# High parts made in the middle of a pair of chunks, and modulation columns one step later, in a three-pass fp32r transformer kernel

## The chip, the cores and the metric

One core of one Trainium2 chip runs the kernel. The metric is device time in microseconds (us); the number before is the median of three runs. Lower is better.

## The reference, cut to what matters

A sequence of 512 rows with 1024 features passes through two hybrid layers, then a pooling layer and a dilated attention layer, each with a gated feed-forward part. All of it is dense fp32 products with small attention parts between them:

```python
mod = c_act @ w_ada + b_ada                 # 6 x 1024 columns: shift, scale, gate, twice
h = modulate(rms_norm(x, norm1_g), shift1, scale1)
(rq, rk, rv, rg, gq, gk, gv, glr, gg, fq, fk, fv, ff) = split(h @ w_in)
ret = silu(rg) * head_group_norm(retention(...))
gla_o = silu(gg) * rms_norm(gla(...))
fox_o = forgetting_attention(rms_norm(fq), rms_norm(fk), fv, ff + b_fox_f)
x = x + gate1 * (sum(gates * y_br) @ w_o)
x = x + gate2 * ((silu(conv(u)) * g) @ w_down)
...
o, lse = dilated_window_attention(q, k, v, window, dilation)    # last layer, 16 heads
```

## The kernel before, in words

**Weights.** They are streamed as numbered chunks of at most 128x1024 fp32 (512 KB). Chunk n uses slot n % 6 of `raw`, `hi` and `lo` (`raw` and `lo` are the same memory). SyncE issues the DMA of chunk n once TensorE (or, for chunks of `w_ada`, VectorE) is done with the earlier chunk in that slot (L2610). ScalarE writes the high part to `hi` (`ScalarSteps.split`, L1211, instruction L1220) after waiting for the DMA to land. GpSimd subtracts to get the low part (L2596). TensorE forms every product in three passes, high x high, high x low, low x high (L427 to L429).

**How far ahead.** Each time the ScalarE program takes a chunk n (`ScalarSteps.chunk`, L1222), it first splits everything up to n + AHEAD, with AHEAD = 4. The split waits in ScalarE's own instruction order: while its DMA is on the way, nothing behind it on ScalarE runs.

**Pairs.** Where rows are wanted instead of columns (values and the gated part's keys), two chunks na and nb = na + 1 are used together (`project_rows`, L479 for TensorE, L1249 for ScalarE). Both slots come free only at the end of the pair. A pair has eight steps of 12 matmuls; the ScalarE part evicts the first bank (`take(0)`) after step four and the second after step eight. A pair can't start in slot 5, so now and then a chunk number is left out. There are 15 pairs, seven in each of the two hybrid layers and one in the last attention layer: two for retention's values, two for the fox values (chunks 45 and 48 in layer 0, 271 and 273 in layer 1), three for the gated part (chunks 50, 52, 54 and 276, 278, 280; `gla_inputs`, L800) and chunk 495 in `attn_inputs` (L1042, ScalarE L1674).

**Order of work.** Every engine runs the same `schedule` (L321) over its own steps. `weave(main, fill)` makes one step of an attention part and then one of a projection. The fox attention has 19 steps n, after four of `fox_norm`; `gla_inputs` is its fill, so the middles of its three pairs fall at n = 0, n = 8 and n = 16, their starts before n = 0, at n = 4 and at n = 12. In a step n TensorE does `score(n)` (L753), `turn(n - 2)` (a transpose of the normalised scores, L764) and, at n = 6, 10, 14 and 18, `value` (L774, instruction L779), which needs ScalarE's copies `foxT` (L1447) up to `turned(n - 3)`. ScalarE does `exp(n)` (L1436), `turned(n - 2)` (L1442), then the fill's step. VectorE does `top(n)` (L2126), then `scale(n - 1)` (L2135, instruction L2140), for which TensorE's `turn` waits. The end of `ret_attention` runs over the first pair of fox values: after the sums (L505) ScalarE takes a root (`rstd`, L1257, instruction L1260), VectorE a reciprocal (L2060), and TensorE spreads it (`head_rows`, L509, instruction L517).

**Modulation.** For columns 4 to 11 of layer 0 and all twelve of layer 1 the product with `w_ada` runs on VectorE beside other work (`VectorSteps.ada`, L1949): four chunks of two multiply-adds (L1965), eight steps in all. After the last come a transpose (L1978) and a sum (L1980) into `AS`. TensorE then folds `AS` into a bank with four small fp32 products (`ada_fold`, L612, instruction L618), and VectorE adds the bias (`ada_add`, L1933, instruction L1938). Both come at the start of the step that begins the next column, and VectorE's first multiply of the next column (L1962) waits for the fold. Banks are taken in a fixed rotation of two, three or four (`take_bank`, L415); the fold takes one turn of it.

Of the kernel before, what the change touches and what calls it, by code (L numbers as in the profile page):

```python
# [21 lines left out]
AHEAD = 4  # L22
# [101 lines left out]
class Mark:  # L124


    def __init__(self, sem, step=1):
        self.sem, self.step, self.n, self.table, self.sure = sem, step, 0, {}, False
# [187 lines left out]
def qk_jobs():  # L316

    return [job for p in range(8) for job in (("aq", p, 128 * p), ("ak", p, 1024 + 128 * p))]


def schedule(P):  # L321
# [15 lines left out]
    for l in range(DEPTH):  # L337
# [4 lines left out]
        ada = (y for q in range(4, 12) for y in P.ada(0, q)) if l == 0 else iter(())  # L342
        P.order = ["b0", "b1"]
        weave(P.ret_attention(l), beside(P.fox_inputs(l), ada, 16))
        P.order = BIG3
        fill = P.gla_inputs(l)
# [3 lines left out]
        fill = chain(P.gated(l, 0), P.mixing(l, 0, (0, 2)))  # L350
        weave(P.gla_attention(l), fill)
        drain(beside(P.gated(l, 1), ada, 8))
        P.order = BIG4
        drain(beside(chain(P.mixing(l, 0, (1,)), *[P.mixing(l, dp, (0, 2, 1)) for dp in (1, 2, 3)]), ada, 26))
        P.mods(l, 1)
        drain(P.out_proj("w_o", l, P.x_norm(2 * l + 1)))
# [40 lines left out]
class TensorSteps(Steps):  # L397


    def __init__(self, e, K):  # L400
        super().__init__(e, K)
        self.free = {b: None for b in K.bank}
        self.order, self.turn = BIG3, 0

    def chunk(self, parts, width, split=True, pair=False, tag=None):
        n = self.next_chunk(pair)
        self.K.chunks[n] = dict(parts=parts, width=width, split=split, tag=tag)
        return n
# [70 lines left out]
    def project_rows(self, ap, c0, keys, freed, rows=None):  # L479

        t, m = self.t, self.m
        na = self.weight(ap, 0, 8, c0, 128, pair=True)
        nb = self.weight(ap, 0, 8, c0 + 128, 128)
        assert nb == na + 1 and na % NSLOT != NSLOT - 1
        hi, lo = self.K.slot_pair(na)
        for u in range(2):
            b = self.take_bank(keys[u])
            for i in range(2):
                r = 2 * u + i
                pick = slice(r * 128, r * 128 + 128) if rows is None else rows(r)  # L490
                terms = [(t["HH"][:, k, pick], t["HL"][:, k, pick], hi[:, :, k, :], lo[:, :, k, :], self.h_ready(k))
                         for k in range(8)]
                done = [] if i == 0 else [keys[u]] + ([("chunk", na), ("chunk", nb)] if u else [])
                yield from self.dot(self.bank[b][:, i * 256:i * 256 + 256], terms, done,
                                    (m.lo.at(na), m.lo.at(nb), self.free[b]))
            self.free[b] = freed(u)
# [108 lines left out]
    def ada(self, l, q_):  # L605
        for g in range(4):
            self.ada_chunk(l, q_, g)
            yield None
            yield None
        self.ada_fold(l, q_)  # L610

    def ada_fold(self, l, q_):  # L612

# [589 lines left out]
class ScalarSteps(Steps):  # L1203
# [43 lines left out]
            take(i)  # L1247

    def project_rows(self, take):  # L1249
        self.chunk(pair=True)  # L1250
        self.chunk()
        for u in range(2):
            for _ in range(4):
                yield None
            take(u)

    def rstd(self, st, n, width, ready, out, key):  # L1257

        self.q.wait_ge(ready)
        self.e.activation(out, st[:, 0:n], ACT.Sqrt, bias=self.t["eps"][:, 0:1], scale=1.0 / width).then_inc(*key)  # L1260
# [413 lines left out]
    def attn_inputs(self):  # L1674
        e, q, m, t = self.e, self.q, self.m, self.t
        jobs = qk_jobs()
        turned = []

        def rope(i):
            name, p, _ = jobs[i]  # L1680
            self.rope((name, p), 32, 64 ** -0.5 if name == "aq" else 1.0, t["aT"][:, i % 2, :],
                      m.vtake.at(*jobs[i - 2][0:2]) if i >= 2 else None, m.vtake.at("cosine", name, p))

        def keep_rows(u):
            key = ("av", 0, u)
            q.wait_ge(m.dense.at(*key))
            e.activation(t["av"][:, 2 * u:2 * u + 2, 0:256],
                         self.bank[self.K.where.get(key, "b0")][:, :].rearrange("p (t c) -> p t c", t=2),
                         ACT.Copy).then_inc(*m.atake.up(key))

        def keep_tile(p):
            out = self.bank[self.K.where.get(("avt", p), "b0")]
            q.wait_ge(m.dense.at("avt", p), m.attn.at("avr", p - 1) if p > 2 else None)
            if p < 3:
                a = e.activation(t["aV"][:, :], out[:, :], ACT.Copy)
            else:
                a = e.activation(t["aV"][:, :].rearrange("p (r l) -> p r l", r=4),
                                 out[:, :].rearrange("p (l r) -> p r l", r=4), ACT.Copy)
            a.then_inc(*m.atake.up(("avt", p)))

        def turn_values():
            for p in turned:
                q.wait_ge(m.attn.at("avr", p))
                e.activation(t["av"][:, :, p * 128:p * 128 + 128],
                             self.bank[self.K.where.get(("avr", p), "b0")][:, :].rearrange("p (t c) -> p t c", t=4),
                             ACT.Copy).then_inc(*m.atake.up(("av", p, 0)))
            turned.clear()

        def begin(i):
            if i < 2:  # L1710
                rope(i)
            else:
                keep_tile(2)
                turned.append(2)

        yield from self.projects(range(3), 6, begin)
        for what, p, *rounds in ATTN_ORDER:
            if what == "vv":
                self.chunk(pair=True)
                self.chunk()  # L1720
                for i in range(8):
                    if i == 5:
                        turn_values()
                    if i % 4 == 3:
                        keep_rows(i // 4)
                    yield 1 if i >= 8 - rounds[1] else 0
                continue
            self.chunk()
            if p > 1:
                turn_values()  # L1730
            yield rounds[0]
            if what == "v":
                keep_tile(p)
                turned.append(p)
            else:
                rope(2 * p + "qk".index(what))
            yield rounds[1]
        turn_values()
# [82 lines left out]
class VectorSteps(Steps):  # L1821


    def __init__(self, e, K):
        super().__init__(e, K)
        self.late = None

    def out_of(self, key):
        return self.bank[self.K.where.get(key, "b0")]
# [119 lines left out]
    def ada(self, l, q_):  # L1949
        e, q, m, t = self.e, self.q, self.m, self.t  # L1950
        AA, CA = t["AA"], t["CA"]
        for g in range(4):
            n = self.next_chunk()
            raw = self.K.raw[:, n % NSLOT, :]
            if n in self.K.chunks:
                q.wait_ge(*self.K.loaded(n))
            for k in range(2):
                kk = 2 * g + k
                done = [("ada", l, q_, kk)] + ([("chunk", n)] if k and g < 3 else [])
                if kk == 0:  # L1960
                    q.wait_ge(m.anorm.at("ca"), m.stat.at("col", *((l, q_ - 1) if q_ else (l - 1, 11))))
                    a = e.tensor_scalar(AA[:, :], raw[:, 0:512], CA[:, 0:1], None, ALU.mult)  # L1962
                else:
                    q.wait_ge(m.vnorm.at("ada", l, q_, kk - 1))
                    a = e.scalar_tensor_tensor(out=AA[:, :], in0=raw[:, k * 512:k * 512 + 512], scalar=CA[:, kk:kk + 1],  # L1965
                                               in1=AA[:, :], op0=ALU.mult, op1=ALU.add)
                a.then_inc(*m.vnorm.up(*done))
            if g == 3:
                self.ada_sums(l, q_, n, raw[:, 0:512])
            yield None  # L1970
            yield None
        self.ada_add(l, q_)

    def ada_sums(self, l, q_, n, room):

        e, q, m, t = self.e, self.q, self.m, self.t
        q.wait_ge(m.vnorm.at("ada", l, q_, 7))
        e.transpose(room, t["AA"][:, :]).then_inc(*m.vnorm.up(("ada", l, q_, "t")))  # L1978
        q.wait_ge(m.vnorm.at("ada", l, q_, "t"))
        e.tensor_reduce(t["AS"][:, :], room.rearrange("p (b i) -> p b i", i=32), AXX, ALU.add).then_inc(  # L1980
            *m.vnorm.up(("ada", l, q_, "s"), ("chunk", n)))

# [863 lines left out]
```

## Time and profile before

| what | value |
|---|---|
| median of 3 runs | 2996.48 us (2991.75 to 2998.78) |
| the profiled execution, own time | 2995.28 us |
| its span in the trace | 2993.5 us |
| TensorE matmul busy | 2936.0 us, 98% of the span |
| VectorE / ScalarE / GpSimd busy | 1071.3 / 1090.1 / 1176.5 us |
| granted TensorE clock | 0.994 of full speed |
| HBM read | 310.61 MB, 104 GB/s over the span |

Times of rows are in microseconds from the span's start, unless marked ns. "PE" is TensorE, "PEld" its weight load, "DVE" VectorE, "ACT" ScalarE, "POOL" GpSimd, "SP" SyncE. L1220 is line 1220 of the kernel. A matmul's end is modelled, so consecutive matmuls overlap in the records.

### The profile page before, as it was taken

How to read it: one execution, taken by the hardware profiler on the slowest of the kernel's cores; microseconds unless marked ns; L12 is line 12 of the kernel's file. 1: busy time of each engine (PE TensorE's matmuls, PEld its weight loads, DVE VectorE, ACT ScalarE, POOL GpSimd, SP SyncE). 2: the span in 40 equal slices, each digit the busy share in tenths (PEclk: the TensorE clock that was granted, in tenths of full speed). 3: DMA queues.
4: the chain of work that ended last, by engine and by line, in shares of the span. 5: the costliest groups of instructions: out<-in, count | busy, mean ns of one | idle time of the engine just before them, and what ended most of it. 6: DMA issues, size and time to landing. Idle time of an engine off the chain costs nothing.

```text
span 2993.5 us, 36662 instructions
## 1 busy us (share of the span) xinstructions
PE 2936.0 (98%) x15563; PEld 2449.8 (82%) x15563; DVE 1071.3 (36%) x1862; ACT 1090.1 (36%) x1657; POOL 1176.5 (39%) x502
## 2 busy tenths in 40 slices
PE   7999999999999999999999999999999999999999
PEld 4877878898888888788898888988888877888887
DVE  2544365256664633232142220342110266521102
ACT  3424433343332433442244332333222266432221
POOL 1432235334445433234434444434444333344442
PEclk9999999999999999999999999999999999999999
DMA  6332244335555422233333333333333322233332
GB/s 214 99 99 64 75 152 154 92 115 188 193 186 177 113 76 59 61 85 95 98 90 101 98 91 97 96 92 98 93 97 97 88 82 67 72 98 94 96 97 73
DMA packets 523799, 315.09 MB, mean 105 GB/s; under 512 B 15954, under 2 KB 496884, under 8 KB 523380
## 3 DMA queue, kind: packets, MB, share of 16 engines
q1 hardware_dynamic: 523636, 312.75, 35.5%
q8 instruction: 123, 2.02, 0.3%
q14 instruction: 40, 0.33, 0.0%
HBM read 310.61 MB, written 2.10 MB: 104 GB/s over the span
## 4 chain that ended last, share of the span: by engine, by line
PE 93%; DVE 3%; DMA 2%; ACT 1%; issue 0%; SPq 0%; DVEq 0%; ACTq 0%
PE b L427 21%; PE b L429 21%; PE b L428 21%; PE o L427 5%; PE o L428 5%; PE o L429 5%; DMA raw<-in_w_in_dram 2%; PE b L468 1%; PE b L469 1%; PE b L470 1%; PE b L586 1%; PE o L779 1%; PE s L662 1%; PE b L957 1%; PE b L958 0%; PE b L959 0%
## 5 line engine op out<-in xcount | busy, mean ns | idle before, releaser
L2596 POOL TENSOR_TENSOR lo<-raw,hi 128x1024 fp32r<-128x1024 f32 (+1 forms) x492 | 1174.4, 2395 | 1778.7 <-ACT hi L1220 1778.0
L427 PE MATMUL b<-HH,hi 128*128 128x512 f32 x1792 | 713.8, 398 | 3.3 <-DVE rq L2008 3.0
L429 PE MATMUL b<-HH,lo 128*128 128x512 f32 x1792 | 699.0, 390 | 0.0
L428 PE MATMUL b<-HL,hi 128*128 128x512 f32 x1792 | 698.6, 390 | 0.0
L1220 ACT ACTIVATE hi<-raw 128x1024 fp32r<-128x1024 f32 (+1 forms) x492 | 508.9, 1039 | 462.1 <-DMA raw<-in_w_down_dram 105.8
L427 PEld LDWEIGHTS b<-HH,hi 128*128 128x128 f32 x1792 | 336.8, 188 | 83.1 <-issue 12.1
L428 PEld LDWEIGHTS b<-HL,hi 128*128 128x128 f32 x1792 | 337.0, 188 | 71.1 <-issue 2.2
L429 PEld LDWEIGHTS b<-HH,lo 128*128 128x128 f32 x1792 | 336.6, 188 | 71.2
L427 PE MATMUL b<-FH,hi 128*128 128x512 f32 (+1 forms) x594 | 218.0, 367 | 0.0
L428 PE MATMUL b<-FL,hi 128*128 128x512 f32 (+1 forms) x594 | 217.1, 365 | 0.0
L429 PE MATMUL b<-FH,lo 128*128 128x512 f32 (+1 forms) x594 | 217.1, 365 | 0.0
L427 PE MATMUL o<-HH,hi 128*128 128x512 f32 x480 | 187.1, 390 | 0.0
L428 PE MATMUL o<-HL,hi 128*128 128x512 f32 x480 | 186.8, 389 | 0.0
L429 PE MATMUL o<-HH,lo 128*128 128x512 f32 x480 | 186.8, 389 | 0.0
L2301 DVE TENSOR_TENSOR CB<-CB,b 128x512 f32<-128x512 f32 x71 | 48.9, 688 | 352.6 <-PE b L429 339.3
L1609 ACT ACTIVATE FH<-CB 128x512 fp32r<-128x512 f32 x88 | 55.6, 632 | 251.3 <-DVE CB L2301 251.3
L427 PE MATMUL b<-hi,HH 128*128 128x256 f32 x480 | 140.9, 294 | 0.0
L1965 DVE SCALAR_TENSOR_TENSOR AA<-raw,CA,AA 128x512 f32<-128x512 f32 x140 | 135.2, 965 | 4.3
L428 PE MATMUL b<-lo,HH 128*128 128x256 f32 x480 | 136.7, 285 | 0.0
L429 PE MATMUL b<-hi,HL 128*128 128x256 f32 x480 | 136.5, 284 | 0.0
L427 PEld LDWEIGHTS b<-FH,hi 128*128 128x128 f32 x594 | 112.0, 189 | 18.1
L429 PEld LDWEIGHTS b<-FH,lo 128*128 128x128 f32 x594 | 112.0, 189 | 18.1
(464 smaller groups left out, 4494.2 us busy)
## 6 DMA issues: line engine op xcount, KB each, us to landing
raw<-in_w_ada_dram SPq DMA_DIRECT2D x96, 512.0 KB, 5.0
raw<-in_w_up_dram SPq DMA_DIRECT2D x88, 512.0 KB, 4.0
raw<-in_w_in_dram SPq DMA_DIRECT2D x80, 512.0 KB, 4.2
raw<-in_w_mg_dram SPq DMA_DIRECT2D x48, 512.0 KB, 3.8
raw<-in_ffn_w_gate_dram SPq DMA_DIRECT2D x44, 512.0 KB, 3.8
raw<-in_ffn_w_up_dram SPq DMA_DIRECT2D x44, 512.0 KB, 3.8
raw<-in_w_down_dram SPq DMA_DIRECT2D x32, 512.0 KB, 4.0
raw<-in_ffn_w_down_dram SPq DMA_DIRECT2D x32, 512.0 KB, 3.9
```

The costliest lines, as they stand in the source:

```text
L427: e.matmul(out, wh, xh, start=start and k == 0, stop=False)
L428: e.matmul(out, wh, xl, start=False, stop=False)
L429: mm = e.matmul(out, wl, xh, start=False, stop=stop and k == last)
L468: e.matmul(out[:, c], hi[:, k, :], t["HH"][:, k, c], start=(k == 0), stop=False)
L469: e.matmul(out[:, c], hi[:, k, :], t["HL"][:, k, c], start=False, stop=False)
L470: mm = e.matmul(out[:, c], lo[:, k, :], t["HH"][:, k, c], start=False, stop=(k == 7))
L586: mm = e.matmul(out[0:1, :], t["CA"][:, kk:kk + 1], raw[:, k * 512:k * 512 + 512], start=(kk == 0), stop=(kk == 7))
L1220: e.activation(t["hi"][:, c % NSLOT, 0:w], K.raw[:, c % NSLOT, 0:w], ACT.Copy).then_inc(*m.hi.up(c))
L1609: e.activation(t["FH"][:, f, :], CB[:, b, :], ACT.Copy).then_inc(*m.atake.up(("fh", i, f)))
L1965: a = e.scalar_tensor_tensor(out=AA[:, :], in0=raw[:, k * 512:k * 512 + 512], scalar=CA[:, kk:kk + 1], in1=AA[:, :], op0=ALU.mult, op1=ALU ...
L2301: e.tensor_tensor(CB[:, b, :], CB[:, b, :], self.out_of(key)[:, :], ALU.mult).then_inc(*m.vtake.up(key))
L2596: e.tensor_tensor(t["lo"][:, s, 0:w], K.raw[:, s, 0:w], t["hi"][:, s, 0:w].bitcast(F32), ALU.subtract).then_inc(*m.lo.up(n))
```

## The change

On ScalarE, `project_rows` and the pair of `attn_inputs` no longer split up to nb + 4 when the pair starts. They split up to nb + 2 at the start, and the rest after the first bank's eviction, in the middle. In `attn_inputs` this is after `turn_values()` at i == 5. The fold and the addition of a modulation column are made one step later, after the first `yield` of the next column; the last column of a layer is folded at its end as before. VectorE's first multiply of a column no longer waits for TensorE's fold of the column before; the sum into `AS` does instead.

```diff
@@ TensorSteps @@
-            yield None
-            yield None
-        self.ada_fold(l, q_)
+            yield None
+            if g == 0:
+                self.ada_last()
+            yield None
+        self.unfolded = (l, q_)
+        if q_ == 11:
+            self.ada_last()
+
+    def ada_last(self):
+
+        if self.unfolded is not None:
+            self.ada_fold(*self.unfolded)
+            self.unfolded = None
@@ ScalarSteps.project_rows @@
-        self.chunk(pair=True)
-        self.chunk()
+        self.next_chunk(pair=True)
+        n = self.next_chunk()
+        self.split(n + AHEAD - 2)
         for u in range(2):
             for _ in range(4):
                 yield None
             take(u)
+            if u == 0:
+                self.split(n + AHEAD)
@@ ScalarSteps.attn_inputs @@
-                self.chunk(pair=True)
-                self.chunk()
+                self.next_chunk(pair=True)
+                n = self.next_chunk()
+                self.split(n + AHEAD - 2)
                 for i in range(8):
                     if i == 5:
                         turn_values()
+                        self.split(n + AHEAD)
@@ VectorSteps.ada: the same ada_last with ada_add, and @@
-                    q.wait_ge(m.anorm.at("ca"), m.stat.at("col", *((l, q_ - 1) if q_ else (l - 1, 11))))
+                    q.wait_ge(m.anorm.at("ca"), m.stat.at("col", 0, 3) if (l, q_) == (0, 4) else
+                              m.vnorm.at("ada", *((l, q_ - 1) if q_ else (l - 1, 11)), "s"))
@@ VectorSteps.ada_sums @@
-        q.wait_ge(m.vnorm.at("ada", l, q_, "t"))
+        q.wait_ge(m.vnorm.at("ada", l, q_, "t"), m.stat.at("col", *((l, q_ - 1) if q_ else (l - 1, 11))))
```

## Rows read from the trace of the kernel before

**Rows 1.** The page: busy time by engine, and the chain that ended last by engine.

```profile
PE 2936.0 (98%) x15563; PEld 2449.8 (82%) x15563; DVE 1071.3 (36%) x1862; ACT 1090.1 (36%) x1657; POOL 1176.5 (39%) x502
...
PE 93%; DVE 3%; DMA 2%; ACT 1%; issue 0%; SPq 0%; DVEq 0%; ACTq 0%
```

**Rows 2.** TensorE's waits: who waited for whom, us in total, times, longest.

```profile
PE o L779 <- ACT foxT L1447: 10.4, 4, 2.7
...
PE t L517 <- DVE retR L2060: 3.4, 2, 2.3
...
PE b L618 <- DVE AS L1980: 2.3, 2, 1.2
PE o L749 <- ACT foxC L1434: 2.1, 2, 1.5
```

**Rows 3.** The chain in time, 254 to 263 us: start, length, what.

```profile
254.00 0.12 PE b L429
...
254.92 5.34 DMA raw<-in_w_in_dram
...
260.28 1.06 ACT hi L1220
...
262.36 0.70 PE o L779
```

**Rows 4.** Timeline around 209 us, ScalarE, then TensorE; idle before in brackets.

```profile
209.53 1.06 ACT L1220 ACTIVATE hi<-raw 128x1024 fp32r<-128x1024 f32 x1 [3.40 <-DMA raw<-in_w_in_dram]
210.49 0.35 ACT L1260 ACTIVATE retR<-t,eps 128x128 f32<-128x128 f32 x1
...
211.88 0.38 PE L517 MATMUL t<-retR,CON 32*128 32x128 f32 x2 [2.26 <-DVE retR L2060]
```

**Rows 5.** Timeline of ScalarE in layer 1, before the second foxC copy.

```profile
1170.61 1.06 ACT L1220 ACTIVATE hi<-raw 128x1024 fp32r<-128x1024 f32 x1 [0.42 <-DMA raw<-in_w_in_dram]
```

**Rows 6.** Timeline of VectorE, then TensorE, at a late fold.

```profile
414.74 0.69 DVE L1980 TENSOR_REDUCE AS<-raw 128x16 f32<-128x512 f32 x1
...
415.48 0.25 PE L618 MATMUL b<-AS,CON 128*32 128x4 f32 x8 [1.23 <-DVE AS L1980]
```

**Rows 7.** Timeline of VectorE, then GpSimd, 258.5 to 265 us.

```profile
262.06 2.50 DVE L2140 TENSOR_SCALAR foxP<-foxP,foxD 128x256 f32<-128x256 f32 x1
...
259.75 4.66 POOL L2596 TENSOR_TENSOR lo<-raw,hi 128x1024 fp32r<-128x1024 f32 x2 [14.82 <-ACT hi L1220]
```

**Rows 8.** Timeline where the splits go, steps n = 0 to 4, 8 to 10, 16 to 18.

```profile
248.28 0.58 ACT L1475 ACTIVATE gk<-b 128x512 f32<-128x512 f32 x1
...
253.86 0.42 DVE L2140 TENSOR_SCALAR foxP<-foxP,foxD 128x384 f32<-128x384 f32 x1
...
254.60 0.29 PE L769 MATMUL t<-CON,foxP 128*128 128x128 f32 x1
...
272.88 0.59 ACT L1484 ACTIVATE gv<-b 128x512 f32<-128x512 f32 x1
...
274.59 0.29 DVE L2140 TENSOR_SCALAR foxP<-foxP,foxD 128x128 f32<-128x128 f32 x1
...
276.25 0.27 PE L769 MATMUL t<-CON,foxP 128*128 128x128 f32 x1
...
298.76 0.59 ACT L1484 ACTIVATE gv<-b 128x512 f32<-128x512 f32 x1
...
301.48 0.59 PE L779 MATMUL o<-foxT,fv 128*128 128x512 f32 x1
```

**Rows 9.** Timeline of the last layer's pair: ScalarE, GpSimd, TensorE.

```profile
2415.34 2.01 ACT L1220 ACTIVATE hi<-raw 128x1024 fp32r<-128x1024 f32 x2
...
2418.48 1.28 ACT L1750 ACT_TABLE_LOAD   x1
...
2416.48 4.88 POOL L2596 TENSOR_TENSOR lo<-raw,hi 128x1024 fp32r<-128x1024 f32 x2 [4.80 <-ACT hi L1220]
...
2422.03 0.33 PE L1117 MATMUL t<-CON,aP 128*128 128x128 f32 x1 [0.22 <-DVE aP L2446]
```

More of the change, by code:

```diff
@@ L608, in ada @@
             yield None
+            if g == 0:
+                self.ada_last()
             yield None
-        self.ada_fold(l, q_)
+        self.unfolded = (l, q_)
[4 more added lines that the diff above has]
+            self.ada_fold(*self.unfolded)
+            self.unfolded = None
     def ada_fold(self, l, q_):
@@ L1826, in __init__ @@
         self.late = None
+        self.unfolded = None
     def out_of(self, key):
@@ L1970, in ada, with ada_last @@
             yield None
+            if g == 0:
+                self.ada_last()
             yield None
-        self.ada_add(l, q_)
+        self.unfolded = (l, q_)
+        if q_ == 11:
+            self.ada_last()
+    def ada_last(self):
+        if self.unfolded is not None:
+            self.ada_add(*self.unfolded)
+            self.unfolded = None
     def ada_sums(self, l, q_, n, room):
```

## The prediction, made before any run of the change

> **What bounds the kernel now.** The first page parts to read are busy time and the chain that ended last. TensorE is busy for 2936.0 of 2993.5 us and holds 93% of the chain [rows 1]. So nothing but time in which TensorE stands still can be won, 57.5 us in all, much of it at the start. The next view is TensorE's waits. Four kinds concern this change: `value` of the fox attention waits for ScalarE's `foxT` (10.4 us in 4 places), the retention spread for a reciprocal (3.4 in 2), the fold for `AS` (2.3 in 2), the second bias product for `foxC` (2.1 in 2) [rows 2].
>
> The chain in time tells what stands behind the first. At 254.9 a weight DMA is issued, at the start of a gated pair; it lands at 260.26, and only then does ScalarE make a high part, and behind it the copy for which TensorE starts late, at 262.36 [rows 3]. ScalarE was not short of time: it stood in order behind a chunk that TensorE needs four chunks later. The same happens at the start of the third pair, and twice in layer 1. At 209.5 it is the root of the retention sums that stands behind such a split: idle for 3.40 us until the DMA landed, a high part, a root of 0.35, a reciprocal, and TensorE 2.26 us late [rows 4]. In layer 1 the first `foxC` copy stands behind the third of three splits, ended at 1171.67 [rows 5]. At 415.48 the fold waited 1.23 us for the sum that VectorE began at 414.74 [rows 6].
>
> **What the change takes away.** The high parts that are moved are needed at the earliest after the pair, so at the pair's start nobody misses them, and in its middle their DMAs have landed. The removed waits:
> - `foxT`: all 10.4 us [rows 2]. The starts of pairs two and three then hold no split.
> - The retention spread: all 3.4 us [rows 2]. Between the sums and the spread TensorE has at least 24 matmuls of the pair, 24 x 0.12 = 2.9 us [rows 3]; root, reciprocal and the way to TensorE take 211.88 - 210.49 = 1.4 [rows 4].
> - The fold: all 2.3 us [rows 2]. It comes a whole step of the projection later, at least 12 matmuls of 0.12 us or more, against waits of at most 1.2.
> - `foxC`: of 2.1 us the longest is 1.5, the other 0.6 [rows 2]. The 0.6 is the copy itself between two uses of one bank and stays. Pair 276 follows a left-out number and must still split one chunk at its start, but it no longer waits for the third: 0.8 goes.
> - A stalled matmul also loses its overlap: the steps in a running chain are 0.12 us [rows 3], a small product is 0.27 long [rows 8], so 0.15 at each of 8 stalls, 1.2.
>
> Together 10.4 + 3.4 + 2.3 + 0.8 + 1.2 = 18.1 us.
>
> **What it adds.** No instruction is new; the same high parts, low parts, folds and DMAs run. SyncE's queue keeps its order and its waits, since a slot is freed by TensorE or VectorE and not by a split. GpSimd's queue keeps its order too. But two high parts, 2.01 us together, and two low parts, 4.88 [rows 9], now fall into the middle. Behind the high parts stand `exp`, `turned` and, through them, VectorE's `scale`; beside the low parts a VectorE operation may be blocked. The row for that: `scale` is 0.42 us long at 253.86 [rows 8] and 2.50 at 262.06, just as long as GpSimd's second low part, of two that ran from 259.75 to 264.41 [rows 7]. I take it that a `scale` that begins inside a low part ends after it.
> - First gated pair (n = 0). The splits follow the copy at 248.28 and end near 250.9, the low parts run from 250.0 to 254.7. The `scale` of 253.86 would end at 254.7 + 0.4 = 255.2, and TensorE wants it at 254.60 [rows 8]: 0.6 us.
> - Second (n = 8). The splits follow the copy at 272.88, the first low part begins near 274.5 and ends near 276.9. The `scale` of 274.59 would end at 277.2, TensorE wants it at 276.25 [rows 8]: 1.0 us. If it slips in ahead of the low part this is 0.1 (`turned` is then late instead). I take 1.0, as row 7 began its operation in the same instant as GpSimd and lost.
> - Third (n = 16). The last `scale` is past. The splits follow the copy at 298.76 and end at 301.3; the last `turned`, 0.6 long, ends at 301.85 and TensorE wants it at 301.48 [rows 8]: 0.35 us.
> - Both layers: 2 x 1.95 = 3.9 us.
> - The last layer's pair. Here the splits at 2415.34 waited for no DMA; nothing is won. They now stand ahead of the table load of 1.28 at 2418.48 [rows 9], at 2418.4 to 2420.4. The first `exp` ends 1.9 us later, at 2422.5. The low parts run from 2419.5 to 2424.4, and VectorE's two scalings (0.5) end at 2425.0, where TensorE wanted them at 2422.03 [rows 9]: 3.0 us. Without the block it would be 1.2. I take 3.0: the scalings would begin well inside.
> - The other eight pairs have no attention in their second half, and no cost if the low parts are in time. The nearest is pair 45: half a pair is 48 x 0.12 = 5.8 us, copy, high part and low part about 4.2. With those 1.6 us of cover gone TensorE would wait for `lo`.
> - The folds. TensorE's work is the same, 0.25 us each [rows 6], 20 of them. They now come at the end of a tile, so VectorE adds the column before it evicts that tile, some 0.5 us later. With three or four banks in turn this is hidden behind the next tile's 24 matmuls. In the stage with two banks the next tile waits for just that eviction: 0.2 us, once. Bounds: nothing, and 20 x 0.25 = 5 us.
>
> **The sum.** -18.1 + 3.9 + 3.0 + 0.2 = -11.0 us. The profiled execution took 2995.28, so 2984.3 for its like; it stands 1.2 under the median of 2996.48, so the forecast for the median is 2985.5 us. The unknown is the cost of the collisions: from below 0, if all of it is hidden (-18.1), from above a whole blocked operation in each of seven pairs.
>
> **A page against the change.** What rows 7 show is one operation. The Trainium skill, SBUF — State Buffer, section "Who interferes with whom", makes a rule of it: VectorE operations in a two-port mode, or with two SBUF inputs, and GpSimd exclude each other for a whole instruction, whoever issues first. By that rule every pair whose middle meets attention pays; that rival is worked out below from rows, and the trace agrees with the rule at 262.06.
>
> **Rivals.**
> 1. All hidden. The moved parts find gaps, as ScalarE idles for over half of its time [rows 1]. -18.1: 2978.4. Against it: `scale` and `turned` have under 1 us of slack at n = 8 and n = 16. Chance 0.13.
> 2. No change. The stall only moves: each of the six gated pairs costs one blocked operation, 2.5 us [rows 7], and the last layer 3.0. 15.0 + 3.0 - 18.1 = -0.1: 2996.4. For it: the moved work is exactly what stood in the way before. Against it: in the third pair no `scale` is left to be blocked. Chance 0.12.
> 3. Slower. Place: the middles of the six gated pairs and of the last layer's. Mechanism: a `scale` starts behind a low part, loses a whole 2.5 us, and the late high part costs its 0.96 besides (half of 2.01 [rows 9]): 7 x 3.5 = 24.5, less 18.1: +6.4, 3002.9. It decides from 18.1 / 7 = 2.6 us a pair on. Against it: where I can place the operations, it is 0.4 to 1.0 in the gated pairs. Chance 0.05.
> 4. The change does only half of what it says: behind ScalarE's wait stands another, such as the transpose or `scale`, that ends nearly as late. Half of 10.4 + 3.4 stays: +6.9 on the forecast, 2992.4. Against it: at 259.5 the transposes before `value` had long run. Chance 0.08.
>
> My forecast has 0.62.
>
> **How the numbers follow.** The likeliest case gives 2985.5, by itself from 2981 to 2990 (collisions between 3 and 11 us; three runs of before lie 7 us apart). The range takes in all hidden below, 2978, and most of the half case above, 2993; no change and slower are left out, 0.17 together. A measurement of this kernel can tell about 0.2%, 6 us: faster means below 2990.5. That is the forecast (0.62), all hidden (0.13) and a part of the half case (0.05): 0.80. Same: the rest of the half case and no change, 0.15. Slower: 0.05.
>
> **What would show each step.** In TensorE's waits the row L779 <- `foxT` should fall from 10.4 to about 1, L618 <- `AS` and L517 <- `retR` should go, L749 <- `foxC` should stand near 1.3. New or longer rows: L769 <- `foxP` some 3 us, L1117 <- `aP` about 3 us more. ScalarE's high parts in the pairs should show no idle time for a DMA in the middle. In the trace of GpSimd and VectorE a `foxP` scaling of about 2.5 us should stand near n = 2 and n = 8. I am wrong if TensorE waits for `lo` after a pair, if the L779 wait stays, or if the last layer's first transpose is late by much more than 3 us.

## The result, and the profile after

The changed kernel takes 2977.02 us (median of 6 runs, 2976.43 to 2977.35), the kernel before in the same comparison 2995.96 (6 runs, 2991.75 to 2998.78): ratio 0.9939, 95% interval [0.9929, 0.9948]. It is faster, by 18.9 us. The forecast was 2985.5, 11 us faster, with a range down to 2978.0: the sign was right, the size was not, and the result lies 1 us outside the range. The runs of after also lie within 1 us of each other, those of before within 7.

First the page of after: the span, the busy times and the chain by engine.

```profile
span 2975.5 us, 36681 instructions
PE 2930.4 (98%) x15563; PEld 2445.2 (82%) x15563; DVE 1065.4 (36%) x1862; ACT 1087.8 (37%) x1657; POOL 1173.9 (39%) x502
PE 95%; DVE 3%; ACT 1%; DMA 1%; issue 0%; SPq 0%; DVEq 0%; ACTq 0%
```

The span fell by 2993.5 - 2975.5 = 18.0 us. Against [rows 1] this splits in two. TensorE stands still for 2975.5 - 2930.4 = 45.1 us instead of 57.5: 12.4 less. And it is busy for 5.6 us less, though it does the same matmuls. The forecast had only the first kind.

TensorE's waits of after (waiting line, releaser, us in total, times, longest), the lines that answer to [rows 2] and two that are new or longer:

```profile
PE t L1128 <- DVE aP L2473: 5.0, 6, 2.4
...
PE t L780 <- DVE foxP L2167: 1.6, 4, 0.6
...
PE o L760 <- ACT foxC L1448: 1.4, 2, 0.7
...
PE o L790 <- ACT foxT L1461: 0.2, 1, 0.2
```

The waits for `retR` and `AS` are gone, `foxT` is 0.2 instead of 10.4, `foxC` 1.4 instead of 2.1. The scales `foxP` cost 1.6 and the last layer's `aP` 5.0, where it was 2.9 before. So the queue did what was forecast. (L1128, L780, L760 and L790 are L1117, L769, L749 and L779 of before.)

Most of the other 5.6 us is in a view that the forecast had not read stretch by stretch: the granted clock. Four stretches of the kernel **before** (window, its length, TensorE busy, weight load, VectorE, ScalarE, GpSimd, then granted clock, DMA share, GB/s):

```profile
212.00:216.00 4.00, 4.00 (x44) 3.77 (x45) 2.29 (x4) 0.00 (x0) 1.01 (x1) 0.57 0.00 0
262.40:266.80 4.40, 4.40 (x14) 3.15 (x15) 2.36 (x2) 1.27 (x4) 2.01 (x1) 0.62 0.00 0
1217.80:1222.40 4.60, 4.58 (x15) 3.49 (x16) 0.68 (x2) 1.32 (x4) 2.28 (x1) 0.65 0.00 0
2502.00:2506.00 4.00, 4.00 (x14) 3.17 (x14) 1.86 (x3) 3.33 (x9) 0.54 (x1) 0.58 0.10 31
```

and the like of the kernel **after**, behind the retention spread, around the third pair's `value` in layer 1, and late in the last layer:

```profile
209.00:213.00 4.00, 4.00 (x72) 3.68 (x62) 2.38 (x4) 0.00 (x0) 0.00 (x0) 1.00 0.00 0
...
1215.00:1219.00 4.00, 4.00 (x20) 3.28 (x19) 0.00 (x0) 0.46 (x1) 0.00 (x0) 1.00 0.76 197
...
2485.00:2489.00 4.00, 4.00 (x13) 2.98 (x11) 1.74 (x3) 2.53 (x7) 1.37 (x1) 0.57 0.00 0
```

A mean of 0.57 over 4.00 us means that TensorE ran most of it at 1.2 GHz, half of its 2.4, and lost 4.00 x (1 - 0.57) = 1.7 us. The other three rows of before give 4.40 x 0.38 = 1.7, 4.60 x 0.35 = 1.6 and 4.00 x 0.42 = 1.7. The first three of the four stretches of before stand directly behind waits that the change removes: the spread released at 211.88, and `value` at 262.36 and in the third pair of layer 1. They are gone; the fourth, which has no long wait ahead of it, is still there. The chain of before shows it step by step:

```profile
214.17 0.21 PE b L428
214.38 0.21 PE b L429
...
215.85 0.12 PE b L427
215.97 0.12 PE b L428
```

The same kind of matmul takes 0.21 us a step until 215.85 and 0.12 from there on.

**The whole account.** Set each matmul of before beside the same one of after. The difference of their starts is the lead of after. It grows and shrinks like this (us):

| place | lead, change of it | forecast |
|---|---|---|
| stalls for `foxT`, four | 2.87 + 2.70 + 2.84 + 3.01 = +11.4 | +11.0 (10.4 and 4 overlaps) |
| stalls for `retR`, two | 2.33 + 1.24 = +3.6 | +3.7 |
| folds, two | 1.3 + 1.1 = +2.4 | +2.6 |
| `foxC` in layer 1 | +0.8 | +0.8 |
| stretches at 1.2 GHz that are gone, three | 1.5 + 1.6 + 1.6 = +4.7 | none |
| middles of the six gated pairs | -0.34 - 0.82 - 0.41 in each layer = -3.1 | -3.9 |
| the last layer's pair | -2.2 | -3.0 |
| `foxC`'s product at 259.65 in layer 0, behind VectorE's `EfL` (ends at 259.60) | -0.2 | none |
| an eviction one bank late | nothing seen | -0.2 |
| the rest, from the start-up and the end | +0.6 | none |
| sum | +18.0 | +11.0 |

This is one execution of each kernel. The mean granted clock is on record for each execution: 0.996 or 0.997 in all six of after, 0.992 to 0.996 with a median of 0.994 in the 39 of before beside the experiments. A difference of 0.002 is 6 us of 2990, known to some 3 us, as the clock is given to three places. So the gain by the clock is no accident of the two traces, though its 4.7 us are measured in these two alone.

### The profile page after: what moved, and what is told of

The parts are those of the page before. It is cut to its first block, busy times and chain, and to the rows that moved or that the text cites. A ratio compares the mean times of both kernels' runs of the same rounds, so it can differ in the third digit from the quotient of the medians.

```text
span 2975.5 us, 36681 instructions
## 1 busy us (share of the span) xinstructions
PE 2930.4 (98%) x15563; PEld 2445.2 (82%) x15563; DVE 1065.4 (36%) x1862; ACT 1087.8 (37%) x1657; POOL 1173.9 (39%) x502
## 4 chain that ended last, share of the span: by engine, by line
PE 95%; DVE 3%; ACT 1%; DMA 1%; issue 0%; SPq 0%; DVEq 0%; ACTq 0%
PE b L428 22%; PE b L430 21%; PE b L429 21%; PE o L428 5%; PE o L430 5%; PE o L429 5%; PE b L469 1%; PE b L470 1%; PE b L471 1%; PE b L587 1%; PE o L790 1%; PE s L673 1%; PE s L770 1%; PE b L968 1%; PE b L970 0%; PE b L969 0%
## 5 line engine op out<-in xcount | busy, mean ns | idle before, releaser
L1983 DVE SCALAR_TENSOR_TENSOR AA<-raw,CA,AA 128x512 f32<-128x512 f32 x140 | 128.7, 919 | 3.8
L429 PEld LDWEIGHTS b<-FL,hi 128*128 128x128 f32 x594 | 112.0, 189 | 18.1
L430 PEld LDWEIGHTS b<-FH,lo 128*128 128x128 f32 x594 | 112.0, 188 | 18.1
```

The costliest lines, as they stand in the source:

```text
L429: e.matmul(out, wh, xl, start=False, stop=False)
L430: mm = e.matmul(out, wl, xh, start=False, stop=stop and k == last)
```

## Experiments

Each kernel is timed against the kernel before on the same chip. The runs came in three groups: e1 to e4 (before: 2994.12 us, 13 runs), e5 to e8 (2995.29, 17 runs), e9 and e10 (2995.12, 9 runs). A stretch "at 1.2 GHz" is read from rows like those above; the long one at the start-up and the one at the end, which all kernels have, are not counted.

### e1: the last layer's pair put back

```diff
-                self.next_chunk(pair=True)
-                n = self.next_chunk()
-                self.split(n + AHEAD - 2)
+                self.chunk(pair=True)
+                self.chunk()
...
                         turn_values()
-                        self.split(n + AHEAD)
```

> The changed kernel with the last layer's pair put back: its two high parts are made at the pair's start again. Theory A (the last layer's part of the change only costs): TensorE's wait L1128 <- aP falls from 5.0 us to about 2.9, the value before the change, and the time is 2 us below the changed kernel's 2977.0, near 2975. Rival B (the wait there only moves, as the stage's end is set by VectorE): no difference, 2977.

Measured 2973.9 us (2971.88 to 2975.71), ratio 0.9925 [0.9911, 0.994]. TensorE waits for `aP` as before:

```profile
PE t L1128 <- DVE aP L2471: 2.9, 6, 0.7
```

The trace has no stretch at 1.2 GHz in the body of the kernel. This part of the change costs time; e9 and e10 measure how much.

### e2: the late split in the pairs of the two hybrid layers only, nothing else

The kernel before with this alone:

```diff
     def project_rows(self, take):
-        self.chunk(pair=True)
-        self.chunk()
+        self.next_chunk(pair=True)
+        n = self.next_chunk()
+        self.split(n + AHEAD - 2)
...
             take(u)
+            if u == 0:
+                self.split(n + AHEAD)
```

> The kernel before, with the late split in project_rows alone (folds and the last layer as before). Theory A: the stalls behind ScalarE go, and with three of them the stretches of TensorE at half clock that followed: waits -13, overlap -1, clock -5, collisions +3, together 16 to 17 us under before, near 2979.5; no stretch at half clock near 212, 263 and 1218 us. Rival B (the 5.6 us by which TensorE is busy for less after the change come with the folds or with the banks, not with the stalls): busy time stays near 2936 and the gain is about 11 us, 2985.

Measured 2975.59 us (2975.29 to 2976.34), ratio 0.9932 [0.9917, 0.9946]: 18.5 us under before where 16 to 17 were expected. The trace has the `foxP` waits of after (1.6 in 4), one fold wait left, and no stretch at 1.2 GHz. TensorE is busy for 2929.7 us, so rival B is out. Beyond the three stretches that were expected to go, the one at 2502 is gone too (1.7 us), and one of the two fold waits (1.2), though the fold was not touched. This one edit is worth as much as the whole change within what these runs can tell.

```profile
PE t L769 <- DVE foxP L2143: 1.6, 4, 0.6
...
PE b L618 <- DVE AS L1983: 1.1, 1, 1.1
```

### e3: the fold one step later, nothing else

The modulation part of the diff on the kernel before; the pairs split as before.

```diff
+            if g == 0:
+                self.ada_last()
             yield None
-        self.ada_fold(l, q_)
+        self.unfolded = (l, q_)
+        if q_ == 11:
+            self.ada_last()
```

> The kernel before, with the fold and the column's addition a step later alone. Theory A: 2.3 us of waits and 0.3 of overlap, 2.6 us under before, and TensorE busy as before (2936): near 2993.4. Rival B (the busy time falls with the folds): 2.6 + 5.6 = 8 us, near 2988.

Measured 2995.8 us (10 runs, 2993.83 to 3000.2), ratio 1.0007 [0.9997, 1.0016]: no gain that can be told. TensorE is busy for 2936.7 us, so the busy time does not fall with the folds (rival B). Both fold waits are gone and matmul by matmul the lead grows by 1.3 and 1.1 us there. But this trace has one stretch at 1.2 GHz more than before's, and it stands behind a stall that both kernels share. Of the kernel before, the chain at the second pair of layer 1:

```profile
1189.21 0.49 ACT foxT L1447
1189.70 0.04 issue
1189.74 2.31 PE o L779 x7
```

and of e3:

```profile
1186.71 0.49 ACT foxT L1458
1187.20 0.04 issue
1187.24 3.88 PE o L790 x6
```

Before: seven `value` products in 2.31 us. In e3: six in 3.88. The clock of e3 ahead of and behind that point:

```profile
1183.00:1187.00 4.00, 1.56 (x11) 1.10 (x9) 0.94 (x5) 2.90 (x5) 2.35 (x2) 1.00 0.37 105
1187.50:1191.50 4.00, 4.00 (x11) 2.28 (x11) 1.95 (x1) 0.56 (x4) 1.80 (x1) 0.57 0.00 0
```

TensorE stood still for 2.4 of these 4 us and was then granted half its clock. The kernel before stood still for 2.5 of 4.6 us in the same place and was granted all of it:

```profile
1185.00:1189.60 4.60, 2.14 (x16) 1.68 (x14) 1.50 (x8) 3.00 (x6) 2.46 (x2) 1.00 0.48 136
1189.60:1193.60 4.00, 3.86 (x21) 2.87 (x21) 3.04 (x2) 1.45 (x5) 2.20 (x1) 1.00 0.00 0
```

The single stall is 2.7 us long in e3 and 2.6 in before. So stalls of almost the same length can be followed by such a stretch or not. That explains the missing 1.7 of the 2.4 us in this one execution; that the median of ten runs gained nothing fits it, and the mean granted clock of the ten (median between 0.993 and 0.994, where before has 0.994) does not speak against it; but the other nine have no trace.

### e4: the late split in the gated pairs only

`project_rows` gets a flag; retention's and the fox's pairs split as before, the gated ones (`keep_k`, `keep_v`) late.

```diff
-    def project_rows(self, take):
+    def project_rows(self, take, late=False):
         self.next_chunk(pair=True)
-        n = self.next_chunk()
-        self.split(n + AHEAD - 2)
+        if late:
+            n = self.next_chunk()
+            self.split(n + AHEAD - 2)
+        else:
+            self.split(self.n - 1 + AHEAD)
+            n = self.next_chunk()
+            self.split(n + AHEAD)
...
-            if u == 0:
+            if u == 0 and late:
```

> The kernel before, with the late split in the three gated pairs of each layer alone (chunks 50, 52, 54, 276, 278, 280); the fox pairs still split at their start. Theory A: the foxT waits go (10.4 + 0.6 of overlap), foxC 0.8, and two of the three stretches at half clock (3.3); collisions +2.7: 12.5 us under before, near 2983.5. The retR waits and the stretch at half clock near 212 us stay. Rival B (no clock in it): 9 us, near 2987.

Measured 2984.07 us (2981.38 to 2985.64), ratio 0.9959 [0.9944, 0.9973]. That is near the 2983.5 expected only because before was faster in this group: the gain is 10.1 us, between the 12.5 of theory A and the 9 of rival B, and does not decide. In the trace `foxT` is gone, the spread's wait is not, and the stretches near 263 and 1218 are gone as theory A has it. But there is a new one, twice as long as the others, at 991:

```profile
PE t L517 <- DVE retR L2068: 3.9, 2, 2.7
```

```profile
987.00:991.00 4.00, 2.22 (x19) 2.05 (x18) 2.21 (x6) 1.43 (x3) 0.00 (x0) 1.00 0.71 246
991.00:997.80 6.80, 6.80 (x34) 6.80 (x33) 0.17 (x1) 0.26 (x1) 0.00 (x0) 0.50 1.09 312
```

It loses 6.80 x 0.50 = 3.4 us. It stands behind a wait of 1.8 us for `X` at the turn to layer 1, which e1 and the change have just as long and pass at full clock.

### e5 and e6: the retention root made late on purpose

Two (e5) or three (e6) ScalarE copies of 128x2048 stand ahead of the root, in the otherwise unchanged after. They write tiles that are free at that point. The edit of e6 (e5's has the first two names):

```diff
+        q.wait_ge(m.stat.at("rsum", l))
+        for name in ("rq", "rk", "retP"):
+            e.activation(t[name][:, :, :], t["retS"][:, :, :], ACT.Copy)
         self.rstd(bank["t1"], 128, 128, m.stat.at("rsum", l), t["retR"][:, :], m.aattn.up(("rsd", l)))
```

> The changed kernel with two extra ScalarE copies of 128x2048 (into memory that nobody reads again) ahead of the root of the retention sums, in both layers. The root is then about 3.6 us later; its cover in the changed kernel is 2.6 us (reciprocal done at 206.81, TensorE's spread at 209.38). Both theories: TensorE waits about 1.0 us in L518 <- retR in each layer, 2 to 2.6 us over the changed kernel, near 2979.5. Theory A (half clock follows only long stalls): no new stretch at half clock. Rival B (any stall can bring one): one or two stretches, 1.7 us each.

> The same with three such copies, so the root is about 5.4 us later and TensorE waits about 2.8 us in each layer, as long as the removed stalls were. Theory A (a removed stall was worth its own length and, at some places, 1.7 us of half clock besides): one or two stretches at half clock of 3.4 us just after the spread (near 212 and 1130 us), TensorE busy for 1.7 us more per stretch, 7.5 to 9.5 us over the changed kernel, near 2985.5. Rival B (the half clock before the change had another cause than the stall): no stretch, 5.9 us over, near 2983.

e5: 2981.02 us (2979.95 to 2982.19), ratio 0.9951 [0.9936, 0.9966], 4.0 over the change, where 2 to 2.6 were expected. e6: 2988.08 (8 runs, 2986.2 to 2990.27), ratio 0.9975 [0.9964, 0.9986], 11.1 over it, where 7.5 to 9.5 were expected by theory A and 5.9 by B. First e5's wait, then e6's:

```profile
PE t L518 <- DVE retR L2090: 2.0, 2, 1.0
```

```profile
PE t L518 <- DVE retR L2090: 5.6, 2, 2.8
```

In e5 the stalls of 1.0 us are followed by full clock in both layers. It has two stretches at 1.2 GHz in the last layer, at 2557 and, behind the late transposes of the last layer's pair (a wait of 2.4 us), at 2407, against the change's one at 2485:

```profile
2407.00:2410.50 3.50, 3.50 (x11) 2.37 (x11) 1.63 (x8) 1.27 (x6) 0.00 (x0) 0.52 0.65 179
```

So 2.0 us of wait and one stretch more, 1.7, make up the 4.0 nearly. Behind the new stalls theory A holds. The trace has the one stretch more that rival B counts, but in another place. In e6 those of 2.8 us are followed by half clock in both layers, and for twice as long as expected; two single stretches stand elsewhere. The one at 2557 in e5 and the ones at 989 and 2566 in e6 stand behind waits of 1.9 us for `YL` and 1.8 for `X`, which the change has too and passes at full clock. e6's clock by stretch:

```profile
211.00:218.00 7.00, 5.92 (x50) 5.70 (x51) 3.68 (x5) 0.04 (x1) 0.00 (x0) 0.51 0.00 0
989.30:992.80 3.50, 3.50 (x20) 3.50 (x19) 0.00 (x0) 0.00 (x0) 0.00 (x0) 0.52 0.78 266
1136.00:1143.00 7.00, 6.35 (x52) 6.12 (x53) 3.32 (x5) 0.00 (x0) 0.00 (x0) 0.51 0.00 0
2566.00:2570.00 4.00, 4.00 (x12) 3.14 (x11) 3.86 (x6) 1.26 (x2) 0.00 (x0) 0.57 0.00 0
```

They lose 7.00 x 0.49 = 3.4, 3.50 x 0.48 = 1.7, 3.4 and 1.7: 10.2 us, against 1.7 in the change. Stalls of 5.6 us in all thus come with 8.5 us more at 1.2 GHz in this execution, 6.8 of them right behind the stalls; that the rest comes from them is not shown. Its span is 13.0 over the change's, so some 1 us of the 14.1 is hidden; the median shows 11.1. Before's own stall at the first spread, 2.3 us [rows 2], was of this kind.

### e7: the late split in the fox's pairs only

The counterpart of e4: the flag of e4's `project_rows` is set for the two pairs of `fox_inputs` in each layer, and for no others.

```diff
-            yield from self.project_rows(take)
+            yield from self.project_rows(take, True)
```

> The kernel before, with the late split in the fox pairs alone (chunks 45, 48, 271, 273); the gated pairs split at their start. Theory A: the retR waits go (3.4 and 0.3 of overlap) and with them the stretch at half clock near 212 us (1.7); the foxT waits stay at about 10.4 and can still bring stretches at half clock: 3.7 to 5.4 us under before, near 2989.5. Rival B (the cover for lo is too short once the split is late): a wait of L427 for lo after pair 45 or 271, gain below 2 us.

Measured 2991.84 us (10 runs, 2985.54 to 2994.54), ratio 0.9984 [0.9975, 0.9994], 3.5 under before: just outside the 3.7 to 5.4 expected. The retention wait is gone, TensorE waits nowhere for `lo` (rival B is out), and `foxT` stays:

```profile
PE o L779 <- ACT foxT L1455: 11.0, 4, 2.9
```

The profiled execution is at the slow end of the ten (2994.54), with five stretches at 1.2 GHz, one of them double. e4 and e7 give 2994.12 - 2984.07 = 10.1 and 3.5 us, 13.5 together; e2, which has both edits and those of retention's value pairs besides, gives 2994.12 - 2975.59 = 18.5. The two are worth more together than one by one. I read this as the clock. The mean granted clock over all executions fits: its median is 0.994 in before, in e4 and in e7, and 0.997 in e2. But the intervals of the times are some 3 us wide or more, and retention's value pairs were not run alone, so it is not shown.

### e8: the two late splits two steps apart

In e1, with one late split behind the first eviction and the other two steps on.

```diff
         for u in range(2):
-            for _ in range(4):
+            for i in range(4):
                 yield None
+                if u == 1 and i == 1:
+                    self.split(n + AHEAD)
             take(u)
             if u == 0:
-                self.split(n + AHEAD)
+                self.split(n + AHEAD - 1)
```

> e1 (the last layer's pair put back) with the two late splits of a pair made apart: one after the first bank's eviction, the other two steps later. Theory A (the loss at n = 0, 8 and 16 comes from two high parts and two low parts in a row): L780 <- foxP falls from 1.6 to below 0.5, the short L790 <- foxT wait goes, 1 to 2.5 us under e1, near 2972. Rival B (one high and one low part are enough to block a scale): the wait of 0.6 us at n = 8 stays and others come at n = 3 or n = 11: within 0.5 us of e1, 2974.

Measured 2974.42 us (2973.82 to 2975.56), ratio 0.9929 [0.9915, 0.9944]: the same as e1. The short `foxT` wait is gone as theory A has it, but the collisions did not shrink, they moved:

```profile
PE t L780 <- DVE foxP L2167: 3.1, 4, 1.0
```

Of GpSimd, then of VectorE, in e8 (start, us, engine, line, operation):

```profile
248.77 2.38 POOL L2623 TENSOR_TENSOR lo<-raw,hi 128x1024 fp32r<-128x1024 f32 x1 [0.83 <-ACT hi L1231]
```

```profile
249.54 1.83 DVE L2167 TENSOR_SCALAR foxP<-foxP,foxD 128x384 f32<-128x384 f32 x1
```

A single low part of 2.38 us is enough to hold a `scale` until it ends (248.77 + 2.38 = 251.15, the scale at 251.37). The theory that the pair of splits is at fault fell; the rival, that one is enough, held.

### e9 and e10: the change and e1 side by side

The change itself once more, and e1's kernel once more, on one chip.

> The change itself once more, beside the kernel in which only the last layer's pair is put back, on one chip, since those two had been timed in different calls (2977.02 and 2973.9 us). Theory A (the last layer's pair costs about 2.2 us of late transposes, and the stretch at 1.2 GHz near 2485 us goes with it, 1.7 us): this kernel lies 2 to 4 us above the other, and its trace has that stretch again. Theory B (the stretch comes and goes with the chip and the execution, and the 3 us between the two were that): the two lie within 1.5 us of each other, and the trace may show no stretch, or one in another place.

> The last layer's pair put back, once more, on the same chip as the change. Theory A: 2 to 4 us below the change, no stretch at 1.2 GHz in the pairs or behind them, the transposes wait 2.9 us in all for the scalings as in the kernel before. Theory B: within 1.5 us of the change.

e9, the change: 2977.25 us (5 runs, 2976.06 to 2978.56), ratio 0.994 [0.9926, 0.9953]. e10: 2974.82 us (5 runs, 2972.69 to 2975.72), ratio 0.993 [0.9918, 0.9943]. The runs don't overlap, the medians lie 2.4 us apart: the last layer's pair is better left as it was. Of e9:

```profile
PE t L1128 <- DVE aP L2473: 5.1, 6, 2.4
```

```profile
2484.00:2488.00 4.00, 4.00 (x12) 3.10 (x12) 1.86 (x3) 2.94 (x8) 0.93 (x1) 0.57 0.02 5
```

Matmul by matmul e9 loses 2.2 us against e10 at the late transposes and 1.6 at 2485; the spans differ by only 2.0, as e10 is 2 us slower in the start-up. The mean granted clock is 0.996 in ten of the eleven executions of the change and 0.997 in seven of the nine of e1's kernel, which fits a stretch more in most executions of the change. That the second loss comes from the first isn't shown: 80 us lie between them, and the kernel before, e3, e4 and e7 have that stretch without the late transposes.

## Why the prediction was wrong in size

**The sum's first half held.** The removed stalls were forecast at 18.1 us and measured 18.2. That `foxT` was late only because the copy stood behind a split, that the retention root is covered, that the fold needs no more than one step, and that 0.6 of `foxC` stays: all as forecast. The root has more room than the forecast's "at least": it is 2.6 us early (e5's expectation) where 2.9 - 1.4 = 1.5 was counted on. The half case (rival 4) and no change (rival 2) are out; `lo` is waited for nowhere.

**A term was missing: the clock, 4.7 us.** The step that failed is "So nothing but time in which TensorE stands still can be won, 57.5 us in all". Of TensorE's busy time some could be won too: it fell by 5.6 us. The page's mean of 0.994 was taken for a constant. It is the mean over a start-up, an end and four stretches at half clock, three of them behind the very stalls that the change removes. The rows were there: 0.57 in 212 to 216, and steps of 0.21 instead of 0.12 us in the chain behind 211.88. e6 puts such stalls back on purpose and gets the stretches back with them; e5, with stalls of 1.0 us, does not. e3 shows the reverse of the argument: 2.4 us of removed stall with nothing to show for it, since a stretch appeared elsewhere. What the runs show is that the stretches went with the stalls; what decides whether a given stall brings one stays open.

**The collisions were sized too high, 6.9 us for 5.3.** The mechanism was right, and at n = 8 the row came as written. VectorE, then GpSimd, of after:

```profile
266.68 2.37 DVE L2167 TENSOR_SCALAR foxP<-foxP,foxD 128x128 f32<-128x128 f32 x1
```

```profile
266.58 4.69 POOL L2623 TENSOR_TENSOR lo<-raw,hi 128x1024 fp32r<-128x1024 f32 x2 [15.93 <-ACT hi L1231]
```

The scale, 0.29 us long in [rows 8], takes 2.37 and TensorE is late by 0.8 by the lead, 0.6 of it in the wait row (forecast 1.0). At n = 0 the low parts ran from 245.85 to 250.65, and the two scales that fell into them lost less:

```profile
247.45 0.95 DVE L2167 TENSOR_SCALAR foxP<-foxP,foxD 128x256 f32<-128x256 f32 x1
...
249.84 1.03 DVE L2167 TENSOR_SCALAR foxP<-foxP,foxD 128x384 f32<-128x384 f32 x1
```

Each waits just for the end of the low part that runs: the second ends at 250.87, GpSimd's at 250.65. The forecast had TensorE 0.6 late, it was 0.34. The low parts themselves were placed right. The copy of [rows 8] at 248.28 stands at 244.25 in after, a lead of 4.0, and the forecast's end of the low parts, 254.7 - 4.0 = 250.7, is the measured one. What failed is the step behind it, "would end at 254.7 + 0.4 = 255.2" (255.1 by its own terms): a blocked scale does not take its whole length again once the low part is over, it ended 0.2 us after it. At n = 8 it is the same: with a lead of 7.9 the scale was to end at 277.2 - 7.9 = 269.3, and it ended at 269.05, some 0.1 after the middle of the two low parts, 266.58 + 4.69 / 2 = 268.9. At n = 16, where no scale is left, TensorE was 0.4 late for 0.35.

The Trainium skill, SBUF — State Buffer, section "Who interferes with whom", says of a VectorE operation in a two-port mode and GpSimd that whoever issues first gets the shared pair of ports for the whole instruction. The rows don't name the mode of the scale. By that rule the wait lies between nothing and one low part, according to where in it the scale starts; the rows above agree, with 0.95, 1.03, 1.83 and 2.37 us for operations of under half a microsecond.

**The last layer's pair: 2.2 us for 3.0.** The chain of after:

```profile
2398.40 1.89 ACT hi L1231 x2
...
2400.31 1.28 ACT L1766
...
2401.60 0.89 ACT aP L1766 x4
...
2402.72 1.69 DVE aP L2473 x2
...
2404.45 0.44 PE t L1128 x2
```

It is the chain that was written down: splits, table load, `exp`, two blocked scalings. Without the block they take 0.49 (e1's chain has that), so it costs 1.2, and the later `exp` the other 1.0. GpSimd's low parts ran from 2399.43 for 4.69 us, to 2404.12. With the lead of 19.75 that is 2423.9 where the forecast had 2424.4, and the scalings ended 0.3 behind them for 0.5: together most of the 0.8 that was too much.

**The side and the rivals.** Rival 3 (slower) decided from 2.6 us a pair on; the gated pairs cost 0.3 to 0.8. Rival 1 (all hidden) gave 2978.4, close to what was measured, but by another way: the collisions are not hidden, their 5.3 us are paid back, 4.7 of them by the clock. A right number from it would have been luck.

## What to carry to other kernels

Put an order that waits for a transfer as far down an engine's program as its consumer allows: with that alone (e2) this kernel gains what the whole change does, and where it buys nothing (the last layer's pair, whose transfer had long landed) it only costs. Before a stall is priced, read the granted clock of the few microseconds behind it, window by window: a mean of 0.994 hid 1.7 us behind each of three stalls, and a saving of one or two microseconds elsewhere can be given back by one such stretch. Moving the low parts by two steps (e8) moved the collision with VectorE, it didn't remove it.

## What the runs showed that I had not expected

- **Half clock behind stalls of two to three microseconds.** TensorE's granted clock fell from 2.4 to 1.2 GHz right behind stalls of 2.3 to 2.8 us (and of 1.8 for `X` in e4, e6 and e7, 1.9 for `YL` in e5 and e6), for 1.7 us lost (0.57 over 4 us), and in e4, e6 and e7 for twice that (0.50 over 6.80 us in e4). It did so behind some of these stalls and not behind others of nearly the same length: near 1187 us 2.6 in before, with 1.00, and 2.7 in e3, with 0.57. Behind stalls of 1.0 us (e5's, at the spread) no trace shows it.
- **It also falls where no long stall is near.** The stretch at 2485 us stands behind a window in which TensorE was busy for 3.67 of 4.00 us. What brings it on stays open.
- **The spread of the runs went with the stalls.** The runs of before lie 5 to 11 us apart in the four comparisons, those of the change, of e2 and of e8 1 to 2.5, those of e1 3 to 4. A stretch more or less, at 1.7 us each, is the likely reason, and the mean granted clock that is on record for each execution bears it out: the seven of before at 0.992 or 0.993 took 2995.1 to 3000.6 us, the ten at 0.995 or 0.996 took 2990.0 to 2995.8. In which places the stretches fell only the traces tell, one for each kernel.
- **A scale waits for one low part, not for both.** At n = 8 the two low parts ran back to back (4.69 us for both), and the scale ended at 269.05, in the middle of them. The next scale, 0.35 us long elsewhere, then waited for the second one and ended at 271.43, GpSimd at 271.27:

```profile
269.82 1.61 DVE L2167 TENSOR_SCALAR foxP<-foxP,foxD 128x256 f32<-128x256 f32 x1
```

- **The fused pass beside them is not held up.** The fused `foxP` pass (L2157) took 0.42 us for 128x256 at 265.95, before GpSimd began, and 0.54 for 128x384 at 268.97, beside it, against 0.56 elsewhere. The two differ in pace: alone, the scale takes 0.29, 0.35, 0.42 and 0.49 us for 128 to 512 columns, 0.07 for each 128 more, the fused pass 0.28, 0.42, 0.56 and 0.69, 0.14 for each 128. Of these two it is the one at twice the pace that GpSimd blocks. That the pace is the reason is not shown.
